# Summing the modulation accumulators over partitions on TensorE instead of by accumulating DMAs, in a two-layer hybrid backbone on one core

## The reference, cut to what matters

```python
sc, scc = silu(c), silu(c_ctx)                      # conditioning vectors, 1024 long: latent and context
h, hc = x, ctx                                      # 256 latent and 256 context tokens of 1024
for l in range(2):
    m  = split(sc  @ w_ada[l] + b_ada[l], 9)        # nine modulation vectors of 1024 for the latent tokens
    mc = split(scc @ w_ada[l] + b_ada[l], 9)        # and nine for the context tokens
    h  = h  + 0.5 * m[2]  * swiglu(modulate(rmsnorm(h,  g1), m[0],  m[1]),  w_in1, w_out1)    # hc alike
    h  = h  + m[5] * mix_out(modulate(rmsnorm(h, gm), m[3], m[4]) @ w_in_mix, scans, ...)     # hc alike
    h  = h  + 0.5 * m[8]  * swiglu(modulate(rmsnorm(h,  g2), m[6],  m[7]),  w_in2, w_out2)    # hc alike
return rmsnorm(h, final_norm_g)
```

## Time and profile before

| | us |
|---|---|
| median of three runs (1570.52 to 1571.65) | 1571.51 |
| the profiled execution | 1571.65 |
| its span in the trace | 1569.9 |
| TensorE matmuls busy | 1550.9 (99%) |
| VectorE busy | 1054.0 (67%) |
| ScalarE busy | 682.6 (43%) |
| GpSimd busy | 159.1 (10%) |

### The profile page before, as it was taken

The page is one execution under the profiler, slowest core; times in us unless marked ns, Lnnn a source line. Parts: engine busy times, 40 slices in busy tenths (PEclk is TensorE's granted clock), DMA queues, the critical chain, the costliest instruction groups (busy, mean ns, idle before and its releaser), DMA issues.

```text
span 1569.9 us, 22187 instructions
## 1 busy us (share of the span) xinstructions
PE 1550.9 (99%) x8796; PEld 1339.8 (85%) x8796; DVE 1054.0 (67%) x1305; ACT 682.6 (43%) x1112; POOL 159.1 (10%) x193
## 2 busy tenths in 40 slices
PE   8999999999999999999999999999999999999997
PEld 6888888889888988888888898888888897999997
DVE  5777874794868567874378477784368578965553
ACT  4434433333784343433233353343332369654452
POOL 0011110022100201110002200011002211000011
PEclk9999999999999999999999999999999999999999
DMA  9577664665322257663367446764367523465562
GB/s 367 198 212 206 201 186 137 206 203 129 107 81 80 82 188 208 199 186 98 121 205 212 114 153 190 217 197 115 98 203 229 154 89 127 135 201 187 188 200 82
DMA packets 79468, 262.53 MB, mean 167 GB/s; under 512 B 13201, under 2 KB 13457, under 8 KB 78353
## 3 DMA queue, kind: packets, MB, share of 16 engines
q1 hardware_dynamic: 71696, 248.70, 49.3%
q0 software_dynamic: 7680, 12.59, 5.0%
HBM read 247.62 MB, written 1.05 MB: 158 GB/s over the span
## 4 chain that ended last, share of the span: by engine, by line
PE 94%; DVE 2%; ACT 1%; DMA 1%; issue 0%; SPq 0%; POOL 0%; POOLq 0%; DVEq 0%; ACTq 0%
PE bank L446 84%; PE bank L568 2%; PE bank L574 2%; PE bank L570 2%; DMA ada_head<-head_w 1%; PE bank L737 1%; PE bank L711 1%; PE bank L709 1%; PE bank L710 1%; PE bank L523 0%; PE bank L739 0%; DVE w_lo L1173 0%; PE bank L462 0%; PE bank L454 0%; DVE l_q L1441 0%
## 5 line engine op out<-in xcount | busy, mean ns | idle before, releaser
L867 ACT ACTIVATE w_hi<-raw 128x1024 fp32r<-128x1024 f32 x317 | 335.9, 1060 | 722.1 <-PE bank L446 707.1
L1173 DVE TENSOR_TENSOR w_lo<-raw,w_hi 128x1024 fp32r<-128x1024 f32 x317 | 388.3, 1226 | 313.3 <-ACT w_hi L867 312.8
L446 PE MATMUL bank<-z_hi,w_hi 128*128 128x512 f32 (+1 forms) x1480 | 537.7, 363 | 1.8 <-DVE w_lo L1173 1.4
L446 PE MATMUL bank<-z_lo,w_hi 128*128 128x512 f32 (+1 forms) x1480 | 534.7, 361 | 0.0
L446 PE MATMUL bank<-z_hi,w_lo 128*128 128x512 f32 (+1 forms) x1480 | 534.5, 361 | 0.0
L446 PEld LDWEIGHTS bank<-z_hi,w_hi 128*128 128x128 f32 x1480 | 278.5, 188 | 46.0 <-DVE w_lo L1173 1.8
L446 PEld LDWEIGHTS bank<-z_hi,w_lo 128*128 128x128 f32 x1480 | 279.8, 189 | 42.4
L446 PEld LDWEIGHTS bank<-z_lo,w_hi 128*128 128x128 f32 x1480 | 278.4, 188 | 42.8 <-issue 1.0
L446 PE MATMUL bank<-h_hi,w_hi 128*128 128x512 f32 (+1 forms) x770 | 267.4, 347 | 0.0
L446 PE MATMUL bank<-h_hi,w_lo 128*128 128x512 f32 (+1 forms) x770 | 266.9, 347 | 0.0
L446 PE MATMUL bank<-h_lo,w_hi 128*128 128x512 f32 (+1 forms) x770 | 266.9, 347 | 0.0
(11 more groups left out here) (187 smaller groups left out, 1405.6 us busy)
## 6 DMA issues: line engine op xcount, KB each, us to landing
raw<-weights SPq DMA_DIRECT2D x320, 512.0 KB, 4.1
ada_raw<-ada_w SPq DMA_DIRECT2D x128, 512.0 KB, 4.3
ada_head<-head_w SPq DMA_DIRECT2D x8, 1024.0 KB, 19.1
up_acc<-up_acc POOLq DMA_DIRECT2D x20, 256.0 KB, 6.5
down_acc<-down_acc POOLq DMA_DIRECT2D x12, 256.0 KB, 6.2
up_acc<-up_acc POOLq DMA_DIRECT2D x40, 64.0 KB, 6.1
res<-x_t SPq DMA_DIRECT2D x4, 512.0 KB, 5.1
down_acc<-down_acc POOLq DMA_DIRECT2D x24, 64.0 KB, 5.5
```

What stands on the lines that cost most here:

```text
L446: m = pe.matmul(bank[:, to], w, x[:, k, at], start=start and i == 0, stop=stop and i == 2, skip_group_check=True)
L867: act.activation(w_hi[:, r, :], raw[:, r, :], ACT.Copy).then_inc(hi_ready, 1)
L1173: dve.tensor_tensor(w_lo[:, r, :], raw[:, r, :], w_hi[:, r, :].bitcast(F32), ALU.subtract).then_inc(lo_ready, 1)
```

## The change

The 128 partitions are summed by matmuls. A new constant `sel` (128 x 2 x 32) has ones in column 0 of its first block and in column 1 of its second. For each vector and stream four matmuls, one for each column group of 32, take `sel[:, stream, :]` as stationary and a quarter of the accumulator (256 columns in runs of 32) as moving operand, and add both streams into one half of `p_ada`: 8 fp32 matmuls a vector. Two vectors of a stage are summed together where there are two (`ring_full`), after the slot that follows their last piece. VectorE transposes the bank once and copies two of each 32 columns into `mods`. The folding DMAs, the quarter transposes, the reductions and ScalarE's small copies go. The stages' shares change from up 4, 3, 3, 0 and down 2, 2, 2, 0 to up 4, 4, 4, 0 and down 2, 1, 1, 0. Counts of semaphores are changed to match.

```diff
-UP_MODS = {(0, 0): 4, (0, 1): 3, (1, 0): 3, (1, 1): 0}
-DOWN_MODS = {(0, 0): 2, (0, 1): 2, (1, 0): 2, (1, 1): 0}
+UP_MODS = {(0, 0): 4, (0, 1): 4, (1, 0): 4, (1, 1): 0}
+DOWN_MODS = {(0, 0): 2, (0, 1): 1, (1, 0): 1, (1, 1): 0}
...
+        def ring_full(at, t):
+            m, k = divmod(t - at["first"], KD)
+            if k or not 1 <= m <= at["mods"] or (m % 2 and m < at["mods"]):
+                return ()
+            return range(at["mod"] + (m - 1) // 2 * 2, at["mod"] + m)
...
+            def ring_sum(at, t):                       # TensorE, after slot t
+                full = ring_full(at, t)
+                if not full:
+                    return
+                pe.wait_ge(mods_ready, MODS0 + full[0])
+                pe.wait_ge(acc_done, acc_count(full[-1], KD - 1, 1))
+                for i, mod in enumerate(full):
+                    w = acc_of(at, mod).rearrange("p s (b j i) -> p s b j i", b=KD, j=4)
+                    for st in range(2):
+                        for j in range(4):
+                            m = pe.matmul(p_ada[32 * j:32 * j + 32, i * 256:i * 256 + 256], sel[:, st, :], w[:, st, :, j, :],
+                                          start=(st == 0), stop=(st == 1), tile_position=(0, 32 * j))
+                m.then_inc(acc_read, len(full))
...
                     if mod >= 2:
-                        act.wait_ge(turned, 4 * (mod - 1))
+                        act.wait_ge(acc_read, mod - 1)
...
-                mod = turn_of(at, t - 1)
-                if mod is not None:
-                    act.wait_ge(summed, mod + 1)
-                    src = ada_sums[:, mod % 4, :].rearrange("p (b j) -> p b j", j=4)
-                    for g in range(4):
-                        rows = slice(mod * KD + 4 * (g // 2), mod * KD + 4 * (g // 2) + 4)
-                        for j in range(4):
-                            act.activation(mods[32 * j:32 * j + 32, rows, g % 2], src[32 * g:32 * g + 32, :, j],
-                                           ACT.Copy).then_inc(mods_ready, 1)
...
-            def ada_turn(at, mod):
-                acc = acc_of(at, mod).rearrange("p s n -> p (s n)")
-                dve.wait_ge(quarters_folded, 64 * (mod + 1))
-                for g in range(4):
-                    own = slice(32 * g, 32 * g + 32)
-                    dve.transpose(ada_turned[own, :, :].rearrange("p b r -> p (b r)"), acc[own, quarter(g)]).then_inc(turned, 1)
-                dve.wait_ge(turned, 4 * (mod + 1))
-                if mod >= 4:
-                    dve.wait_ge(mods_ready, MODS0 + 16 * (mod - 3))
-                dve.tensor_reduce(ada_sums[:, mod % 4, :], ada_turned[:], AX_X, ALU.add).then_inc(summed, 1)
+            def ada_turn(mod, n):
+                dve.wait_ge(mods_ready, MODS0 + mod)
+                dve.transpose(ada_turned[:, 0:n * KD, :].rearrange("p b r -> p (b r)"), p_ada[:, 0:n * 256]).then_inc(turned, n)
+                dve.wait_ge(turned, mod + n)
+                dve.tensor_copy(mods[:, mod * KD:(mod + n) * KD, :], ada_turned[:, 0:n * KD, 0:2]).then_inc(mods_ready, n)
...
-            def fold(at, mod):                         # GpSimd's queue, and its 16 calls
...
+            pool.memset(sel[:], 0.0)
             link(pool.memset(ident[:], 0.0))
+            for s in range(2):
+                pool.memset(sel[:, s, s:s + 1], 1.0)
```

More of the change, by code:

```diff
@@ L631, in up_stage @@
                         slot(t // 4, t % 4)
+                        ring_sum(at, t)
                 else:
@@ L656, in row @@
                         m.then_inc(slot_done, 1)
+                        if len(ss) == 2:
+                            ring_sum(at, q)
                 def row_by_stream(d):
@@ L726, in in_stage @@
                             pe.wait_ge(bd_zero, l + 1)
+                            pe.wait_ge(mods_ready, MODS0 + AT["norm", n]["mod"])
                         if u == 1 and sets == 2:
@@ L1356, in ring_turn @@
             def ring_turn(at, t):
-                mod = turn_of(at, t)
-                if mod is not None:
-                    ada_turn(at, mod)
+                full = ring_full(at, t - 1)
+                if full:
+                    dve.wait_ge(acc_read, full[-1] + 1)
+                    ada_turn(full[0], len(full))
             def up_stage(l, f):
@@ L1695, in prep_gate @@
                                    ALU.mult).then_inc(prepped, 1)
-            def fold(at, mod):
-                acc = acc_of(at, mod)
-                low, high = slice(0, 64), slice(64, P)
-                pool.wait_ge(acc_done, acc_count(mod, KD - 1, 1))
-                pool.dma_start(acc[low, :, 0:512], acc[high, :, 0:512], accum_op=ALU.add).then_inc(halves_folded, 16)
-                pool.dma_start(acc[high, :, 512:D], acc[low, :, 512:D], accum_op=ALU.add).then_inc(halves_folded, 16)
-                pool.wait_ge(halves_folded, 32 * (mod + 1))
-                acc = acc.rearrange("p s n -> p (s n)")
-                for g in range(4):
-                    own, other = slice(32 * g, 32 * g + 32), slice(32 * (g ^ 1), 32 * (g ^ 1) + 32)
-                    pool.dma_start(acc[own, quarter(g)], acc[other, quarter(g)], accum_op=ALU.add).then_inc(quarters_folded, 16)
             def norm(n):
                 w = dft(n)
-                down = AT[(n - 1) // 3, "down", (n - 1) % 3 // 2] if n % 3 != 2 and n else None
                 for d in range(1, 1 + pool_sums(n) - pool_sums(n - 1) if n not in (0, 3 * DEPTH - 1) else 1):
@@ L1718, in norm @@
                     pool.tensor_tensor(scr[:, 2, 0:w], scr[:, 2, 0:w], scr[:, d % 2, 0:w], ALU.add).then_inc(sqsum_ready, 1)
-                    if down is not None and d in FOLD_AT[:down["mods"]]:
-                        fold(down, down["mod"] + FOLD_AT.index(d))
                 if n == 3 * DEPTH:
@@ L1767, in _ @@
             for l in range(DEPTH):
-                up = AT[l, "up", 0]
-                for m in range(3):
-                    fold(up, up["mod"] + m)
                 prep_gate(l, 0)
                 prep_norm(l, 1)
-                for m in range(3, up["mods"]):
-                    fold(up, up["mod"] + m)
                 norm(3 * l + 1)
@@ L1780, in _ @@
                 norm(3 * l + 2)
-                up = AT[l, "up", 1]
-                for m in range(up["mods"]):
-                    fold(up, up["mod"] + m)
                 prep_gate(l, 2)
```

22 lines of the change are left out of this document (5 added, 17 removed).

## The result

| | before | after |
|---|---|---|
| median of 7 runs each, us | 1570.83 (1563.60 to 1571.91) | 1577.54 (1576.68 to 1584.80) |
| ratio | | 1.0065, 95% interval 1.0045 to 1.0087 |
| span of the profiled execution, us | 1569.9 | 1575.5 |

The change makes the kernel slower, but by less than was forecast: by 6.7 us if the two medians are compared and by some 10 us if the ratio is, against 17.0. The two measures differ because the median of 7 hides a second thing: both kernels have two groups of times, 7 us apart. Before: 1563.6 and 1564.6 against 1570.5 to 1571.9 (five of seven). After: 1576.7 to 1577.5 (four of seven) against 1584.1 to 1584.8. Within a group the change costs 13 us.

What follows compares the result with a forecast made beforehand. TensorE was taken as the bound, busy 99%, so added matmuls are paid in full and removed work returns 0. Rounds 13.6 plus entries 3.4 make 17.0 us on 1571.65; forecast 1588.6 us, range 1584.5 to 1594.

Steps and rivals of the forecast that it cites:

- The bunches on TensorE: Nine groups of summing matmuls between slots: 64 rounds of 0.2125 us, 13.6, plus nine entries of 0.38, 3.4; sum 17.0 us.
- Rivals 1 and 2: Bunches: 1, column groups share something at long stretches, 1593, chance 0.10; 2, groups run one after the other, 1629, chance 0.04.
- The new waits: ScalarE, VectorE and SyncE wait for bunches, ScalarE 0.6 us at the tightest place; cost on TensorE 0.
- I take 0 for all of this: Removed folding DMAs, transposes, reductions and small copies of 16 vectors return nothing, since nobody on TensorE waited for them.
- below 0: Low end for the removed work: matmuls slowed beside the folding DMAs, 0.23 us for each of 16 folds, 3.6 us back.
- rival 3: Removed DMAs and copies had slowed L446; a quarter of 74 us over 4650 records returns, 1571; chance 0.06.
- The base, "1571.65 + 17.0": Starting time: profiled execution 1571.65 us, 0.14 over the median 1571.51; with 17.0 added, 1588.65.
- Rival 1: Bunches' column groups under fourfold: by the skill's 3.07x, rounds 17.8 us and sum 21.2; chance 0.10.

Runs made afterwards that it cites:

- the run without folds: Kernel before without its 96 accumulating folding DMAs, transposes, reductions and small copies kept: lower group 1559.7 to 1560.9 us, ratio over all runs 0.9974.
- the one with one matmul: Changed kernel with one fp32 matmul of one column group in each of the nine bunches in place of 16 or 8: 1567.0 to 1568.1 us.
- the 1024-byte pad: Kernel before with an unused tile of 1024 bytes a partition ahead of `scr`: 1563.7 to 1565.1 us.
- turn first: Changed kernel, but VectorE transposes and reduces before TensorE adds the four partition groups: 1574.0 to 1579.6 us; with every tile in its old place 1562.7 to 1564.9.
- the 64-byte pad: Kernel before with an unused tile of 64 bytes a partition ahead of `scr`: 1570.5 to 1571.3 us (3 runs) and 1575.2, 1575.8 (2).
- the 48 short DMAs: Changed kernel plus 48 accumulating DMAs of 4 rows each from GpSimd's queue near the start: lower-group median 1578.4 us.
- the one with one DMA: Changed kernel plus one unneeded accumulating DMA on GpSimd's queue near the start and a new 64-byte tile behind `sel`: 1582.9 to 1587.5 us.

## Why the prediction was wrong

- **The bunches on TensorE: right.** 17.0 us forecast, 17.2 measured; an entry of some 0.38 us and four groups at once hold at 256 columns. Rivals 1 and 2 are out: a bunch of two took 2.1 us, not 3 or 7.
- **The new waits: right.** 0 on TensorE; 0.41 us on ScalarE at the tightest place, 1.2 us in all.
- **"I take 0 for all of this": the step of the mechanism that failed.** The prediction asked of each removed instruction who waited for it on TensorE, and found nobody. The 96 folding DMAs had a price in another place: each lengthens GpSimd's closing drain by 0.082 us, 7.9 in all, of which some 3 lay beside the output's DMA and 4.4 to 4.6 ended the program. That is a term of -4.4 us where the sum has 0. The rows shown did not contain the program's last 8 us, although the chain of waits ends in them, at GpSimd's closing line. For VectorE's and ScalarE's share of the removed work the 0 was right, to within the 1 us to which the sums close. The low end kept for "below 0", 3.6 us, rested on slower matmuls (rival 3), which the run without folds rules out; and it was left out of the stated range.
- **The base, "1571.65 + 17.0": the larger miss, 7 us.** 17.2 less the drain is 13 us, and 13 on 1571.5 would have been 1584.5, at the low edge of the range. The measured median is 1577.5, since the three runs before were all of the upper group and the seven after fell four to three into the lower one. One run more in the upper group would have made the median 1584 and hidden most of the error: on which side of the gap the median fell was chance. Three runs from 1570.5 to 1571.7 looked like a spread of 0.07%. The trace had a sign of it: in the last two stages the 256-column matmuls start 117.8 ns apart all through, while those of 512 columns in the rings start 226.7 apart, twice 113.3. The prediction took 0.229 us from a stretch of the head and did not ask about the stages in which a matmul of half the columns took 4.5 ns more than half the time.
- **Rival 3, given back,** had the wrong mechanism (the matmuls of the rings start 226.7 ns apart with the DMAs and without), but a part of the sum did come back. Its 74 us also rest on the head's 0.229; by 0.2267 they are 66. Rival 1's 17.8 and 21.2 us come out as 17.7 and 21.1. Neither slip moves the forecast.
- **What stays open:** what draws one of the two paces in a run, with every tile in its place. The traces show where it is drawn. All enter the last up stage 118 ns apart. Some (the changed kernel, the one with one matmul, the 1024-byte pad) change to 113.3 within four matmuls, with a few slower ones where the loop begins. Others (turn first, the 64-byte pad, the 48 short DMAs) keep 118 for 72 matmuls and change at the first slot of the loop. The kernel before, the one without folds and the one with one DMA never change in their traces. What tips it was not found.

## What to carry to other kernels

A DMA is not free only because nobody waits for it, and so its removal can return time: look at the end of the program too, at the drain of the queue that issued it. When a median has two groups behind it, compare within the groups, and read the pace of the matmuls in equal stretches before giving a difference to a change. When a change adds a tile, keep the others in their places, or try the shift by itself first: 64 bytes cost this kernel 6.4 us, as much as the difference of the medians that was to be explained.

## What the runs showed of the hardware that was not expected

- The closing drain of GpSimd grows by 0.082 us for each accumulating DMA that its queue issued, at 48 and 96 DMAs (5.30 and 9.22 us; one: 1.45; none: 1.36). 64 rows and 4 rows gave the same, and with 64 rows they were issued over 1360 us ahead of the drain.
- Weight products of 256 columns start 113.3, 117.8 or 120.0 ns apart in the last two stages, and those of 512 columns 226.7, 228.9 or 233 ns, at granted clock 1.00 in every one of these stretches. Which of them came followed the place of the tiles in SBUF (64 and 896 bytes changed it in the down stages, 1024 did not), and in the last two stages it also varied from run to run.
- Four fp32 matmuls of 32 output rows, 128 deep, in four column groups run fully at once at 64 and at 256 moving columns: a bunch of 8 rounds of 0.2125 us costs 2.09 us. Above its rounds a bunch costs 0.36 to 0.42 us when it breaks a stream of 128x128 products. With 16 to 64 columns a bunch of two rounds costs 0.46 to 0.59 us in all.
